# Counting stashed PSUM banks in the order in which ScalarE copies them (gate stage of a hybrid decoder layer)

## What is computed

```python
proj = h @ w_in
gq, gk, gv, gg, glr, hq, hf, hi, hg, ma, mb = jnp.split(proj, idx, axis=-1)
y_a = (rmsnorm(o_a, gla_norm_w) * silu(heads(gg, 4))).reshape(B, T, 1024)
y_b = (rmsnorm(o_b, hgrn_norm_w) * silu(heads(hg, 8))).reshape(B, T, 1024)
merged = sigmoid(ma) * y_a + sigmoid(mb) * y_b
out = merged @ w_out
```

## Time and profile before

| | us |
|---|---|
| median of 3 runs | 879.98 (879.85 to 880.09) |
| the profiled execution's own time | 880.04 |
| its span on the core | 878.3 |
| TensorE busy in the span | 858.7 (98%) |
| VectorE busy | 602.7 (69%) |
| ScalarE busy | 489.2 (56%) |
| GpSimd busy | 251.3 (29%) |

### The profile page before, as it was taken

How to read it: one execution, slowest core, us unless ns; L and a number is a source line. 1 busy time by engine, 2 the same in 40 slices (tenths; PEclk the granted TensorE clock), 3 DMA queues, 4 the chain that set the end, 5 groups by cost and what they waited for, 6 DMA issues and landing times.

```text
span 878.3 us, 12718 instructions
## 1 busy us (share of the span) xinstructions
PE 858.7 (98%) x4688; PEld 711.0 (81%) x4688; DVE 602.7 (69%) x779; ACT 489.2 (56%) x740; POOL 251.3 (29%) x227
## 2 busy tenths in 40 slices
PE   7999899999999999999999999999999999999997
PEld 6777788888888888888887888888888888888885
DVE  3598878669867867784955456844444444599995
ACT  4576465477657666846756543633333333366574
POOL 2123679532141240430443000211111111534200
PEclk9999999999999999999999999999999999999999
DMA  9996497365546445545235931433333336499912
GB/s 338 348 323 134 104 192 112 82 181 154 148 135 175 122 143 148 141 148 152 86 97 168 167 97 49 121 96 98 98 98 99 98 100 233 106 269 206 234 37 96
DMA packets 149235, 130.21 MB, mean 148 GB/s; under 512 B 4743, under 2 KB 132065, under 8 KB 148928
## 3 DMA queue, kind: packets, MB, share of 16 engines
q1 hardware_dynamic: 136048, 110.84, 41.7%
q0 software_dynamic: 13136, 18.69, 12.6%
HBM read 125.31 MB, written 4.20 MB: 147 GB/s over the span
## 4 chain that ended last, share of the span: by engine, by line
PE 73%; ACT 1%; DVE 1%; issue 0%; ACTq 0%
PE ps L2219 17%; PE ps L2220 17%; PE ps L2221 17%; PE ps L2647 4%; PE ps L2648 4%; PE ps L2646 4%; PE ps L2386 1%; PE ps L2541 1%; PE ps L2542 1%; PE ps L2545 1%; PE ps L2366 1%; PE ps L2388 1%; PE ps L2350 1%; PE ps L2353 1%; PE ps L2398 0%; PE ps L2335 0%
## 5 line engine op out<-in xcount | busy, mean ns | idle before, releaser
L2219 PE MATMUL ps<-h_hi,w_hi 128*128 128x512 f32 (+1 forms) x568 | 223.6, 394 | 0.4 <-DVE w_lo L1851 0.4
L2221 PE MATMUL ps<-h_hi,w_lo 128*128 128x512 f32 (+1 forms) x568 | 219.8, 387 | 0.0
L2220 PE MATMUL ps<-h_lo,w_hi 128*128 128x512 f32 (+1 forms) x568 | 219.6, 387 | 0.0
L2219 PEld LDWEIGHTS ps<-h_hi,w_hi 128*128 128x128 f32 x568 | 106.7, 188 | 23.1 <-issue 1.0
L2220 PEld LDWEIGHTS ps<-h_lo,w_hi 128*128 128x128 f32 x568 | 106.8, 188 | 22.0 <-issue 1.0
L2221 PEld LDWEIGHTS ps<-h_hi,w_lo 128*128 128x128 f32 x568 | 106.7, 188 | 21.7
L983 POOL TENSOR_TENSOR prod<-conv 128x512 f32 x21 | 43.2, 2059 | 220.2 <-DVE conv L2061 220.2
L1383 ACT ACTIVATE conv<-ps,vecs 128x512 f32<-128x512 f32 x42 | 32.5, 777 | 132.2 <-PE ps L2221 123.7
L2057 DVE SCALAR_TENSOR_TENSOR conv<-ps,vecs,conv 128x511 f32<-128x511 f32 x44 | 33.0, 749 | 104.8 <-ACT conv L1383 102.4
L1851 DVE TENSOR_TENSOR w_lo<-raw,w_hi 128x1024 fp32r<-128x1024 f32 x46 | 58.8, 1291 | 56.6 <-ACT w_hi L1025 56.6
L1510 DVE TENSOR_TENSOR w_lo<-raw,w_hi 128x1024 fp32r<-128x1024 f32 x52 | 63.9, 1232 | 1.9 <-ACT w_hi L1017 1.8
(11 more groups left out here) (313 smaller groups left out, 1813.0 us busy)
## 6 DMA issues: line engine op xcount, KB each, us to landing
raw<-in_w_in_dram SPq DMA_DIRECT2D x44, 512.0 KB, 3.9
raw<-in_w_up_dram SPq DMA_DIRECT2D x44, 512.0 KB, 3.8
ada_w<-in_w_ada_dram SPq DMA_DIRECT2D x32, 512.0 KB, 4.5
ada_w<-in_w_ada_dram SPq DMA_DIRECT2D x8, 1024.0 KB, 9.4
g_blocks<-in_w_in_dram SPq DMA_DIRECT2D x24, 256.0 KB, 6.1
hres<-in_w_down_dram POOLq DMA_DIRECT2D x12, 512.0 KB, 8.7
raw<-in_w_down_dram SPq DMA_DIRECT2D x11, 512.0 KB, 5.0
raw<-in_w_out_dram SPq DMA_DIRECT2D x8, 512.0 KB, 5.7
```

The costliest lines, as they stand in the source:

```text
L2219: pe.matmul(dst, a_hi, b_hi, start=start and i == 0, stop=False)
L2220: pe.matmul(dst, a_hi, b_lo, start=False, stop=False)
L2221: last = pe.matmul(dst, a_lo, b_hi, start=False, stop=stop and i == n - 1)
```

## The change

`g_stash` counts in the order of `STASH_AT`'s steps and no longer in that of `G_PASSES`.

```diff
 def g_stash(q, p):
-    return 2 * [at for at in G_PASSES if at[1] in G_STASHED].index((q, p))
+    return 2 * [STASH_AT[j] for j in sorted(STASH_AT)].index((q, p))
```

## The result

The changed kernel took 873.53 us (median of four executions, 873.23 to 875.07) against 880.00 of the kernel before: a ratio of 0.993, interval 0.9913 to 0.9947. The changed kernel's profiled execution took 875.07 us, and its trace follows the forecast; the other three took 873.23 to 873.57. So there are two things to explain: the 5.0 us, which can be read from the two traces, and 1.5 more, which cannot be read from them.

A forecast was written before the change was run, and what follows sets the result against it. TensorE, busy 858.7 of 878.3 us, was taken to bound the kernel. Closing its two gate-stage gaps takes 5.01 us from the profiled 880.04, giving 875.03, or 875.0 from the median, with no other loss; range 874.0 to 877.0.

The forecast's parts named there:

- The surplus copy: Gate stage: ahead of (0,GS4) and (0,GS3) TensorE waits for one ScalarE stash copy more than it needs.
- The size of the gaps: TensorE's two gate-stage gaps cost 5.01 us start to start: 1.33 before (0,GS4), 3.55 before (0,GS3), 0.12 in restart.
- (c): VectorE's fold of (0,GS4) drops its surplus wait and moves 1.89 us forward, with the work queued behind it.
- the slack: How early VectorE's folds would be ready for the earlier TensorE: 1.36 us in time at (0,GA22); (1,GA22) needs 2.01 forward.
- Rival 1: VectorE doesn't come forward, through collisions with GpSimd; 2.01 us lost at (1,GA22), 877.0 us; chance 0.16 whole or part.
- the bounds of 1.89 and 5.01: Limits in us for how far VectorE's later work, up to the fold of (1,GS3), shifts forward.
- (e): Count for (1,G11) rises from 4 to 8; TensorE asks ahead of (1,GS2) with 17 us to spare, costing nothing.
- Rivals 2 and 4: Time returns later through waits for weights, or the constants miss the binding waits; 880.0 us each, chance together 0.06.
- holds no warm-up: PEclk stays 1.00 in the longer gate-stage gap, so closing it gives back no half-clock time beyond its length.
- the lower end of the range: 874.0 us, allowing 0.6 for small waits, 0.26 for faster passes and 0.1 for scatter.
- The 0.26: Allowance in us if (0,GS4) and (0,GS3) run at 5.47 us rather than 5.58.
- The 0.1 for scatter: Allowance in us in the range for scatter between runs, which was 0.24 us over three.

The follow-up runs named there:

- the repeated run: Kernel before, unchanged, executed and profiled once more: seven executions at 879.68 to 880.36 us, four at 881.41 to 881.62.

## Why the prediction was right in its mechanism and wrong in its number

- **The surplus copy** held: both gaps ended with a copy that TensorE didn't need, and both are gone.
- **The size of the gaps**, 5.01 us from start to start, held: 91.44 rather than 96.39 for (1,G21), 4.97 in the profiled executions' own times. How it divides between the gaps was beside the point: the first alone is worth nothing, the second alone 3.5 (878.75 with the gap filled, 875.29 with it closed), since the first only brings TensorE sooner to the second.
- **(c), VectorE 1.89 us forward**, held to the hundredth, 90.74 to 88.85, and it was needed. The run with VectorE's old counts lost 1.4 us at exactly the two places for which the slack was worked out.
- **Rival 1**: VectorE had to be 2.01 us forward at the fold of (1,GS3) and was 2.97, inside the bounds of 1.89 and 5.01. The collisions with GpSimd did not eat it up, though there were some: the low parts at 96.77 and 100.62 took 1.76 and 1.75 us.
- **(e), the raised count**, cost nothing: the copy ends at 90.74, (1,GS2) starts some 17 us later. Rivals 2 and 4 fell with the trace.
- **The step that failed** is the sum's "holds no warm-up", together with the lower end of the range. From one trace, in which PEclk stayed at 1.00 in the gap, I concluded that the gap costs only its length. The row was the wrong one for that, since the clock reads 1.00 in the gap of the repeated run too and falls a microsecond behind it. In the first trace it stays at 1.00 behind the gap as well (90.69 to 94 us), but that execution had its fall at the start, the 0.50 at 12 to 14 us of the earlier trace rows, and the sum took that half clock to be the same before and after. The runs bore out neither reading: 63 of 64 executions of the kernel before have a fall at one place at least, by their mean clock, and the changed kernel, without the gap, has none in four of nine. A fall of the common length costs 1.5 to 1.8 us, and three of the first four executions of the changed kernel were without one: hence 6.5 rather than 5.0. The Trainium skill ("TensorE: Matmul & The Clock Gate", Part 1: The HAM clock gate), which says that an idle TensorE falls back to half clock, was right against my reading, and I had written down what it would give: more than the gap. How often it comes to that, only the further executions showed.
- **Smaller terms.** The 0.26 in the lower end of the range should be 0.22, twice 5.58 - 5.47, and 5.47 is the length of (2,G11). The 0.1 for scatter came from three executions within 0.24 us; further ones of the same kernel lie between 878.29 and 881.72.
- **The median** mixes levels. Taken level by level the change is worth what was forecast: 880.04 against 875.07 in the two executions that were profiled with the fall at the start, 878.29 against 873.2 to 873.6 without any. Taken over all, the kernel before loses its fall in the gap as well: the mean of its 64 executions is 880.6, that of the changed kernel's nine is 874.3, 6.3 us apart. The measured 6.5 also has the chance of four draws in it; the changed kernel's second median was 875.01, and 875.0 was forecast. That hit would have been luck: 880.0 before and 875.0 after hold one fall each, and the forecast reckoned with neither as something that comes and goes.

## What to carry to other kernels

Where a count stands for an event, write it in the order in which the waiting is served, not in that in which the work is planned: a count that is too high looks like a dependency in every trace. The wrong order made one count too low as well: 4 for (1,G11), whose copy is the fourth. It did no harm only because TensorE and VectorE had each waited for 8 before, by the surplus count of (0,GS2). So such counts have to be put right together. Gaps in a row are not additive: close the last one first, and see what the earlier ones are worth then. A gap in TensorE can cost more than its length, and whether it does varies from one execution to the next, so look at the times and mean clocks of many executions, and at the durations of the first matmuls, before trusting one profile; where the idle time can't be removed, filling it with matmuls that nobody reads got the clock's share back in both places tried here.

## What the runs showed that I had not expected

A gap of 3.3 us on TensorE was followed by half clock in some executions of one kernel and not in others: with the start filled, nine of eleven had it, and eight of ten with VectorE's counts changed. A gap of 1.2 us was not in any of four. At the start five of nine executions of the changed kernel had it, and none of five with six more fillings. The idle time there was 1.97 to 2.30 us in the profiled executions with a fall and 1.58 in the one without; whether it was shorter in the others without a fall too isn't known, as they weren't profiled. With the start's idle time filled as well, the changed kernel's executions lie within 0.5 us of each other (873.34 to 873.86) instead of 2.0. How the two places of the kernel before hang together, with only one of 64 executions free of any fall although the start alone is spared in four of nine and the gap alone in four of 21, was not tried.
